# Group norm by tile, its first weight slab split in the last chunk, and low halves of the normed outputs on GpSimd

## The chip, the cores and the metric

The kernel runs on one core of a Trainium2 chip. The metric is the device time of one execution in microseconds. Before the change three runs gave 1732.81, 1736.08 and 1736.42 us, a median of 1736.08 us.

## The reference, cut to what matters

A two-layer decoder trunk over 272 tokens (16 learned meta tokens and 256 of text) of 1024 features: sliding-window attention and a dense SwiGLU, then RWKV-7 time mixing and a top-2-of-8 mixture of experts; a layer norm follows each of the four. The change concerns the end of the RWKV-7 mixer:

```
y = wkv7_scan(r, decay, k, v, -kk, kk * a)          # 16 heads of 64
mu_y  = mean(y, -1); var_y = mean((y - mu_y)^2, -1) # per head and token
y = ((y - mu_y) * rsqrt(var_y + GN_EPS)).reshape(B, L, D)
y = y * lnx_g + lnx_b
bonus = sum(r * k * r_k, -1) * v
return ((y + bonus) * g) @ w_o
```

Only the 256 text tokens are needed from here on. All values are float32, and the output is held to float32 accuracy.

## The kernel before, in words

**Layout.** Features lie on the 128 partitions in 8 tiles (`KC`); a tile of the text tokens is 128 x 256. One tile holds two heads. Weights come in slabs of 128 x 2048 (1 MB, 16 tiles of 128 x 128) through a ring of 7 slots in SBUF, which SyncE's queue fills in order (L413); slot n % 7 is loaded again once `slab_taken` says that slab n was split.

**Products in three parts.** A weight slab and the activations are each split in a rounded high half (`_hi`, type float32r) and a low half (`_lo`, the value less its high half). For each slab ScalarE makes `w_hi` by a copy (`round_slab`), VectorE makes `w_lo` by a subtraction (`split_slab`), both in two buffers (n % 2), and TensorE (`products`) runs for each of the 16 tiles w_hi with x_hi and w_hi with x_lo, then waits for `w_lo` and runs w_lo with x_hi for the 16 tiles. That is 48 matmuls of a slab. `linear` walks over the slabs of a square 1024 x 1024 product: 4 slabs, each with two output tiles m and the 8 input tiles k of each, in the order m, then k. For m = 0 it waits for the low half of input tile k before it is used. The same `linear` serves the attention's output projection.

**The recurrence.** RWKV-7 runs over 5 chunks (16 tokens, then four times 64). `recurrence_order()` writes out by hand, once for all engines, the order of the products (TensorE, counted by `c_pe`), of the steps on VectorE (`c_dve`), the copies out of PSUM on ScalarE (`c_act`) and the masks on GpSimd (`c_pool`); the arrays PT, DV, AV and PV give each step's count. The parts of a chunk are "first", five "level" (the doubling of a triangular inverse), "x", "sa", "y" and "s"; the last chunk has "bonus0" and "bonus1" between "x", "sa" and "y" and no "s". The parts of one chunk's end and of the next one's start alternate. Each part works in halves of four tiles (g = 0, 1). The output y is written over the tensor `r_`, the bonus times v into `z`, and the gate g lies in `g_`. `w_hi` and `w_lo` lie over buffers of the recurrence, so a slab can be rounded only once the chunks are done with these.

**Group norm and output projection, before.** After the last copy of y, in this order:
1. ScalarE rounds slab `SL_O2`, VectorE splits it; meanwhile TensorE makes the per-head means of all 8 tiles (`head_sums`, L795, 8 matmuls, one increment).
2. VectorE subtracts the means from all of y in one instruction of 128 x 2048; ScalarE squares all of it in one (L1297); TensorE sums the squares of each head in 8 matmuls with 16 output rows (`head_rows`, L802).
3. VectorE adds epsilon on 16 x 256 (L1713), ScalarE takes the root (L1299), VectorE the reciprocal (L1715); TensorE spreads the 16 rows to all features in 8 matmuls that read 16 rows (`rows_to_features`, L808, one increment at the end).
4. For each tile k, VectorE multiplies by the weight and the spread root (L1721), adds the bias and the bonus (L1723), multiplies by the gate, and makes the low half of tile k - 1; ScalarE makes the high halves (L1303). TensorE starts `linear` on `SL_O2` as tiles come.
5. The residual, the layer norm, the router and the experts follow, all behind this product.

In the profile TensorE matmul instructions of float32 operands have two records each; those of float32r have one.

Of the kernel before, what the change touches and what calls it, by code (L numbers as in the profile page):

```python
# [149 lines left out]
GN_OUT = 3  # L150
# [9 lines left out]
def build(nc, A, OUT):  # L160
    ctx = ExitStack()
    with ctx:
# [124 lines left out]
        b_ra, k_ra, bk_nat = pair[0:2], pair[2:4], pair[4:6]  # L287
        mrb, ltm = [x[:, 0] for x in b_ra], [x[:, 1] for x in b_ra]
# [99 lines left out]
        gn_dve, gn_act, gn_pe = sem("gn_vector_steps"), sem("gn_scalar_steps"), sem("gn_sums")  # L388
        rt_pe, rt_dve, rt_act = sem("router_products"), sem("router_vector_steps"), sem("router_scalar_steps")
# [45 lines left out]
        def _(pool):  # L435
# [50 lines left out]
            for part, c, *level in order:  # L486
# [38 lines left out]
        def _(pe):  # L525
# [20 lines left out]
            def linear(base, outs, chunks, x_hi, x_lo, ready, kept=None, before_out=0, cols=slice(0, T)):  # L546


                for n in range(base, base + outs * chunks // TILES):
                    tiles = [divmod((n - base) * TILES + t, chunks) for t in range(TILES)]  # L550

                    def before(t):
                        m, k = tiles[t]
                        if k == 0 and kept is not None and m + before_out >= 8:
                            pe.wait_ge(kept, m + before_out - 7)
                        if m == 0:
# [3 lines left out]
                                           for t, (m, k) in enumerate(tiles)], before=before)  # L560
# [230 lines left out]
            def head_sums(square, x, wait, value, done):  # L791

                pe.wait_ge(wait, value)
                for m in range(KC):
                    mm = pe.matmul(PS[:, m, TEXT], square, x(m), start=True, stop=True)  # L795
                mm.then_inc(done, 1)

            def head_rows(wait, value, done):

                pe.wait_ge(wait, value)  # L800
                for m in range(KC):
                    mm = pe.matmul(PS[0:HEADS, 0, TEXT], to_head[:, m, :], sq[:, m, TEXT], start=m == 0, stop=m == KC - 1)  # L802
                mm.then_inc(done, 1)

            def rows_to_features(wait, value, done):
                pe.wait_ge(wait, value)
                for m in range(KC):
                    mm = pe.matmul(PS[:, m, TEXT], from_head[:, m, :], rstd[0:HEADS, TEXT], start=True, stop=True)  # L808
                mm.then_inc(done, 1)
# [131 lines left out]

            pe.wait_ge(c_dve, len(DV))
            head_sums(mean_head[:, :], lambda m: r_[:, m, TEXT], c_act, len(AV), gn_pe)
            head_rows(gn_act, 1, gn_pe)
            rows_to_features(gn_dve, 3, gn_pe)
# [144 lines left out]
        def _(act):  # L1090
# [177 lines left out]
            for part, c, *level in order:  # L1268
# [9 lines left out]
                for g in range(2):  # L1278
# [12 lines left out]
                    kept = kept + 1  # L1291
            assert kept == len(AV)
            act.wait_ge(c_dve, len(DV))
            act.wait_ge(c_pe, len(PT))
# [3 lines left out]
            act.wait_ge(gn_dve, 2)  # L1298
            act.activation(rstd[0:HEADS, TEXT], rstd[0:HEADS, TEXT], ACT.Sqrt).then_inc(gn_act, 1)  # L1299
            round_slab(SL_O2 + 1)  # L1300
            for k in range(KC):
                act.wait_ge(gn_dve, GN_OUT + 3 * (k + 1))
# [78 lines left out]
        def _(dve):  # L1381
# [254 lines left out]
            steps = []  # L1636

# [13 lines left out]
            for part, c, *level in order:  # L1651
# [35 lines left out]
                elif part == "level":  # L1687
                    kinds = slice(0, 2) if i < len(levels_of(c)) - 1 else slice(1, 2)
                    for g in range(2):
# [4 lines left out]
                                ALU.add))  # L1694
                elif part[:-1] == "bonus":
# [3 lines left out]
                    step(tt(z[:, 4 * i:4 * i + 4, TEXT], PS[:, 0:4, TEXT], v_[:, 4 * i:4 * i + 4, TEXT]))  # L1699
                elif part == "s":  # L1700
# [3 lines left out]
            dve.wait_ge(c_dve, len(DV))  # L1704

            s = Steps(gn_dve)
            y = r_[:, :, TEXT]
            dve.wait_ge(c_pe, len(PT))
# [284 lines left out]
```

## Time and profile before

| | |
|---|---|
| median of three runs | 1736.08 us (1732.81 to 1736.42) |
| the profiled execution | 1734.36 us, with a span of 1732.6 us |
| TensorE matmul, busy | 1634.2 us (94%), 12050 records |
| VectorE busy | 1289.9 us (74%) |
| ScalarE busy | 999.6 us (58%) |
| GpSimd busy | 92.8 us (5%) |
| granted TensorE clock, mean | 0.962 |
| from the last y product to the layer norm behind the output projection | 628.3 to 690.2 us in the span |
| the experts | from about 734 us to the end |

The share of busy time is a mean over very different stages. The stage that the change touches takes some 62 us of the span; it has to be read by itself, in the table of stretches and in the chain of waits.

### The profile page before, as it was taken

To read this page: it belongs to the slowest core of one execution; us is meant where nothing else is said; L and a number is where in the kernel's file an instruction comes from. 1 tells how busy PE (TensorE), PEld (TensorE's weight loads), DVE (VectorE), ACT (ScalarE), POOL (GpSimd) and SP (SyncE) were. 2 spreads that over 40 slices of the span, in tenths; PEclk is the share of its full clock that TensorE was granted. 3 is DMA by queue.
4 is the path that set the end of the run, shared out by engine and by line. 5 is a ranking of instruction groups with operands and counts; after the bars stand their busy time and mean duration, and the time that the engine had idled before them with its cause. 6 is when DMAs were issued, how large, how long until landed. Compare 5 with 4: busy or idle time off the path is not lost.

```text
span 1732.6 us, 29765 instructions
## 1 busy us (share of the span) xinstructions
PE 1634.2 (94%) x12050; PEld 1288.7 (74%) x12050; DVE 1289.9 (74%) x1260; ACT 999.6 (58%) x1037; POOL 92.8 (5%) x125
## 2 busy tenths in 40 slices
PE   7998999979999977799999999999999999999995
PEld 5787999949889967677777777776777777777774
DVE  3755554466744444789899898998998998998984
ACT  3645443336512221577777777777777777777773
POOL 3310000000023400000000000000000000000000
PEclk9988999989899987799999999999999999999997
DMA  9432454513300002179999999999999999999980
GB/s 260 179 122 99 175 182 185 200 49 119 126 3 4 4 26 76 55 298 369 371 359 366 371 360 371 361 367 369 359 371 373 354 369 369 361 370 360 370 315 26
DMA packets 60291, 425.40 MB, mean 246 GB/s; under 512 B 6887, under 2 KB 8023, under 8 KB 9224
## 3 DMA queue, kind: packets, MB, share of 16 engines
q1 hardware_dynamic: 58152, 416.52, 63.3%
q0 software_dynamic: 2016, 7.13, 1.6%
q8 instruction: 90, 1.47, 0.3%
q14 instruction: 33, 0.27, 0.0%
HBM read 422.28 MB, written 1.12 MB: 244 GB/s over the span
## 4 chain that ended last, share of the span: by engine, by line
PE 71%; DVE 3%; ACT 2%; issue 1%; ACTq 0%; DVEq 0%
PE PS L530 54%; PE PS L817 5%; PE PS L531 4%; PE PS L1035 1%; PE PS L836 1%; PE PS L991 1%; PE PS L845 1%; DVE arena L1396 1%; PE PS L570 1%; PE PS L1021 0%; PE PS L1022 0%; PE PS L576 0%; PE PS L808 0%; PE PS L959 0%; PE PS L802 0%
## 5 line engine op out<-in xcount | busy, mean ns | idle before, releaser
L1396 DVE TENSOR_TENSOR w_lo<-ring,w_hi 128x2048 fp32r<-128x2048 f32 x391 | 894.2, 2288 | 200.3 <-ACT w_hi L1325 88.1
L1325 ACT ACTIVATE w_hi<-ring 128x2048 fp32r<-128x2048 f32 x336 | 644.6, 1919 | 264.3 <-PE PS L530 241.7
L530 PE MATMUL PS<-w_hi,x_hi 128*96 128x512 f32 x896 | 353.9, 395 | 0.7 <-ACT x_hi L1317 0.7
L530 PE MATMUL PS<-w_hi,x_lo 128*96 128x512 f32 x896 | 352.5, 393 | 0.0
L530 PE MATMUL PS<-w_lo,x_hi 128*96 128x512 f32 x896 | 243.0, 392 | 0.0
L1096 ACT ACTIVATE w_hi<-ring 128x2048 fp32r<-128x2048 f32 x55 | 105.3, 1914 | 168.2 <-issue 89.9
L530 PEld LDWEIGHTS PS<-w_lo,x_hi 128*96 128x96 f32 x896 | 144.6, 161 | 62.1
L530 PEld LDWEIGHTS PS<-w_hi,x_lo 128*96 128x96 f32 x896 | 144.8, 162 | 58.5
L530 PEld LDWEIGHTS PS<-w_hi,x_hi 128*96 128x96 f32 x896 | 144.6, 161 | 57.9 <-ACT x_hi L1317 1.0
L530 PE MATMUL PS<-w_hi,hid_hi 128*96 128x512 f32 x448 | 176.7, 394 | 0.0
L530 PE MATMUL PS<-w_hi,hid_lo 128*96 128x512 f32 x448 | 176.0, 393 | 0.0
L530 PE MATMUL PS<-w_lo,hid_hi 128*96 128x512 f32 x448 | 121.9, 394 | 0.0
L817 PE MATMUL PS<-arena 64*64 64x64 f32 (+4 forms) x3296 | 104.1, 216 | 6.2 <-DVE arena L1396 2.3
L1290 ACT ACTIVATE arena<-PS 128x256 f32<-128x256 f32 (+2 forms) x82 | 31.8, 393 | 135.4 <-PE PS L817 83.5
L817 PEld LDWEIGHTS PS<-arena 64*64 64x64 f32 (+2 forms) x3296 | 98.2, 131 | 11.4 <-issue 6.3
L531 PE MATMUL PS<-h_hi,w_hi 128*128 128x272 f32 x352 | 91.9, 295 | 6.8 <-DVE h_lo L1396 6.8
L1396 DVE TENSOR_TENSOR arena<-arena,PS 128x272 f32<-128x272 f32 (+6 forms) x102 | 54.3, 534 | 56.2 <-PE PS L817 53.9
L530 PEld LDWEIGHTS PS<-w_lo,hid_hi 128*96 128x96 f32 x448 | 72.2, 161 | 31.7
L530 PEld LDWEIGHTS PS<-w_hi,hid_hi 128*96 128x96 f32 x448 | 72.2, 161 | 30.8
L530 PEld LDWEIGHTS PS<-w_hi,hid_lo 128*96 128x96 f32 x448 | 72.3, 161 | 30.7
L531 PE MATMUL PS<-h_lo,w_hi 128*128 128x272 f32 x352 | 91.3, 292 | 0.0
L1396 DVE TENSOR_TENSOR experts<-experts,PS 96x512 f32<-96x512 f32 (+1 forms) x113 | 76.0, 673 | 0.0
(261 smaller groups left out, 2051.8 us busy)
## 6 DMA issues: line engine op xcount, KB each, us to landing
ring<-in_slabs SPq DMA_DIRECT2D x395, 1024.0 KB, 4.9
arena<-in_lora POOLq DMA_DIRECT2D x1, 1152.0 KB, 5.4
h<-in_h SPq DMA_DIRECT2D x1, 1088.0 KB, 5.2
arena<-bias_lines POOLq DMA_DIRECT2D x1, 1056.0 KB, 19.6
arena<-bias_lines POOLq DMA_DIRECT2D x1, 1040.0 KB, 24.1
arena<-in_lora POOLq DMA_DIRECT2D x1, 1024.0 KB, 11.9
out<-h SPq DMA_DIRECT2D x1, 1024.0 KB, 4.7
arena<-in_lora POOLq DMA_DIRECT2D x1, 512.0 KB, 6.5
```

Of the source, the lines that this page charges most:

```text
L530: return pe.matmul(out, x, w, start=start, stop=stop) if tokens_stay else \
L531: pe.matmul(out, w, x, start=start, stop=stop)
L570: mm = pe.matmul(PS[:, 0, cols], ones_d[:, :], z[:, k, cols], start=k == 0, stop=k == KC - 1)
L817: mm = pe.matmul(PS[64 * p:64 * p + n_out, b + g, at:at + width], lhsT(m, p), rhs(m, p), start=i == 0, stop=i == len(pairs) - 1)
L836: mm = pe.matmul(out[64 * p:64 * p + CH, :, 0:n], rows_of(x, c)(m, p), r_kk[64 * p:64 * p + 64, :, T * m + START[c]:T * m + START[c] + n], ...
L845: mm = pe.matmul(PS[64 * p:64 * p + CH, b + g, col + CH * (m % 4):col + CH * (m % 4 + 1)], x(m, p), masks[64 * p:64 * p + 64, MASKS.index( ...
L991: mm = pe.matmul(PS[:, 2 * (j % 4) + i, 0:HALF], rows[:, t, P * k:P * k + P], pick[:, t, 4 * half:4 * half + 4, :].rearrange("p e c -> p ( ...
L1035: mm = pe.transpose(PS[:, 4 + g % 2, CAP * j:CAP * (j + 1)], hid_rows[0:CAP, g % 2, P * j:P * (j + 1)], eye[0:CAP, 0:CAP])
L1096: act.activation(w_hi[:, n % 2, :], ring[:, n % SLOTS, :], ACT.Copy).then_inc(hi_set, 1)
L1290: act.activation(out, rows, ACT.Copy).then_inc(c_act, 1)
L1325: act.activation(w_hi[:, n % 2, :], ring[:, n % SLOTS, :], ACT.Copy).then_inc(hi_set, 1)
L1396: tt = lambda o, a, b, op=ALU.mult: dve.tensor_tensor(out=o, in0=a, in1=b, op=op)
```

## The change

On **TensorE**, `head_sums`, `head_rows` and `rows_to_features` become one function `group_norm`: the mean of tile m waits only for its half of y and signals by itself; the sum of squares takes each tile as it is squared; the spreading signals tile by tile. `linear` takes the tiles of a product's first slab in the order k, then m, where the product has fewer than 16 input tiles (this holds for the attention's output projection too). On **ScalarE**, slab `SL_O2` is rounded in quarters after the copies of the last three levels of the last chunk; the squares are taken tile by tile. On **VectorE**, `SL_O2` is split after the last level of the last chunk; (bonus + lnx_b) * g is made in place in `z` right behind each bonus step; the means are subtracted tile by tile; for each tile there are two instructions in place of four: gated y times weight times root, and the sum with `z`. The split of `SL_O2 + 1` moves behind the last of them. On **GpSimd** there are 8 products y * g (into `gated_y`, over the space of `kk`) and 8 subtractions for the low halves `out_lo`.

```diff
@@ pool, behind the recurrence @@
+            for m in range(KC):
+                pool.wait_ge(gn_dve, GN_NORMED + m)
+                pool.tensor_tensor(out=gated_y[:, m, TEXT], in0=r_[:, m, TEXT], in1=g_[:, m, TEXT], op=ALU.mult)\
+                    .then_inc(gn_pool, 1)
+            for k in range(KC):
+                pool.wait_ge(gn_dve, gn_out(k))
+                pool.wait_ge(out_hi_set, k + 1)
+                pool.tensor_tensor(out=out_lo[:, k, TEXT], in0=r_[:, k, TEXT], in1=out_hi[:, k, TEXT].bitcast(F32),
+                                   op=ALU.subtract).then_inc(out_split, 1)
             pool.wait_ge(slab_used, SL_MOE)
@@ tensor, linear @@
-                    tiles = [divmod((n - base) * TILES + t, chunks) for t in range(TILES)]
+                    tiles = [(t, *divmod((n - base) * TILES + t, chunks)) for t in range(TILES)]
+                    if n == base and chunks < TILES:
+                        tiles.sort(key=lambda x: (x[2], x[1]))
@@ tensor, in place of head_sums, head_rows, rows_to_features @@
+            def group_norm():
+                pe.wait_ge(c_dve, len(DV))
                 for m in range(KC):
+                    pe.wait_ge(c_act, AV["y", N_CH - 1, 0, m // 4])
+                    pe.matmul(PS[:, m, TEXT], mean_head[:, :], r_[:, m, TEXT], start=True, stop=True).then_inc(gn_pe, 1)
                 for m in range(KC):
+                    pe.wait_ge(gn_act, m + 1)
                     mm = pe.matmul(PS[0:HEADS, 0, TEXT], to_head[:, m, :], sq[:, m, TEXT], start=m == 0, stop=m == KC - 1)
+                mm.then_inc(gn_pe, 1)
+                pe.wait_ge(gn_dve, GN_ROOT)
                 for m in range(KC):
+                    pe.matmul(PS[:, m, TEXT], from_head[:, m, :], rstd[0:HEADS, TEXT], start=True, stop=True)\
+                        .then_inc(gn_pe, 1)
...
+            group_norm()
+            pe.wait_ge(gn_dve, gn_scaled(1))
             linear(SL_O2, 8, KC, lambda k: out_hi[:, k, TEXT], lambda k: out_lo[:, k, TEXT], (out_split, lambda k: k + 1),
@@ scalar @@
+                if part == "level" and c == N_CH - 1 and i >= 2:
+                    act.wait_ge(c_pe, PT["s", N_CH - 2, 0, 1])
+                    for j in ((), (), (0, 1), (2,), (3,))[i]:
+                        round_quarter(SL_O2, j)
...
-            round_slab(SL_O2)
-            act.wait_ge(gn_dve, 1)
-            act.activation(sq[:, :, TEXT], r_[:, :, TEXT], ACT.Square).then_inc(gn_act, 1)
+            for m in range(KC):
+                act.wait_ge(gn_dve, GN_NORMED + m)
+                act.activation(sq[:, m, TEXT], r_[:, m, TEXT], ACT.Square).then_inc(gn_act, 1)
@@ vector @@
+            def gated_bonus(i):
+                dve.wait_ge(c_dve, DV["bonus", N_CH - 1, i, 0])
+                for m in range(4 * i, 4 * i + 4):
+                    gn.mark(dve.scalar_tensor_tensor(out=z[:, m, TEXT], in0=z[:, m, TEXT], scalar=v_of("lnx_b", m),
+                                                     in1=g_[:, m, TEXT], op0=ALU.add, op1=ALU.mult))
...
+                    if c == N_CH - 1 and i == len(levels_of(c)) - 1:
+                        dve.wait_ge(c_pe, PT["u", c, i, 1])
+                        split_slab(SL_O2)
...
+                    gated_bonus(i)
...
-            split_slab(SL_O2)
-            dve.wait_ge(gn_pe, 1)
-            s.step(tt(y, y, PS[:, :, TEXT], ALU.subtract))
+            for m in range(KC):
+                dve.wait_ge(gn_pe, m + 1)
+                gn.mark(tt(r_[:, m, TEXT], r_[:, m, TEXT], PS[:, m, TEXT], ALU.subtract))
...
+            def scale(k):
+                dve.wait_ge(gn_pool, k + 1)
+                dve.wait_ge(gn_pe, KC + 2 + k)
+                gn.mark(dve.scalar_tensor_tensor(out=r_[:, k, TEXT], in0=gated_y[:, k, TEXT], scalar=v_of("lnx_g", k),
+                                                 in1=PS[:, k, TEXT], op0=ALU.mult, op1=ALU.mult))
+            scale(0)
+            for k in range(KC):
+                if k + 1 < KC:
+                    scale(k + 1)
+                dve.wait_ge(gn_dve, gn_scaled(k))
+                gn.mark(tt(r_[:, k, TEXT], r_[:, k, TEXT], z[:, k, TEXT], ALU.add))
             split_slab(SL_O2 + 1)
-            for k in range(KC):
-                yk = r_[:, k, TEXT]
-                s.step(dve.scalar_tensor_tensor(out=yk, in0=yk, scalar=v_of("lnx_g", k), in1=PS[:, k, TEXT],
-                                                op0=ALU.mult, op1=ALU.mult))
-                s.step(dve.scalar_tensor_tensor(out=yk, in0=yk, scalar=v_of("lnx_b", k), in1=z[:, k, TEXT],
-                                                op0=ALU.add, op1=ALU.add))
-                s.mark(tt(yk, yk, g_[:, k, TEXT]))
-                if k:
-                    dve.wait_ge(gn_dve, s.n - 3)
-                    left(out_lo[:, k - 1, TEXT], r_[:, k - 1, TEXT], out_hi[:, k - 1, TEXT], out_hi_set, k, out_split)
```

## Rows read from the trace of the kernel before

**Rows 1.** Stretches: length; busy PE, PEld, DVE, ACT, POOL; granted clock; DMA share; GB/s.
```profile
628.00:633.00 5.00, 3.96 (x26) 3.08 (x22) 2.30 (x2) 2.18 (x2) 0.00 (x0) 1.00 0.00 0
633.00:637.00 4.00, 0.00 (x0) 0.00 (x0) 2.18 (x1) 1.78 (x1) 0.00 (x0) 0.89 0.67 236
...
646.40:653.60 7.20, 7.16 (x16) 5.14 (x16) 2.29 (x1) 0.01 (x1) 0.00 (x0) 0.50 0.42 146
653.60:667.10 13.50, 4.78 (x13) 3.01 (x12) 12.85 (x31) 3.24 (x8) 0.00 (x0) 0.50 0.00 0
667.10:671.10 4.00, 3.96 (x20) 3.82 (x21) 0.43 (x1) 0.10 (x1) 0.00 (x0) 0.60 0.00 0
671.10:690.20 19.10, 19.10 (x163) 19.10 (x162) 6.66 (x8) 3.83 (x2) 0.00 (x0) 1.00 0.31 111
900.00:1700.00 800.00, 800.00 (x3630) 566.06 (x3628) 727.66 (x454) 577.97 (x381) 0.00 (x0) 1.00 0.94 358
```

**Rows 2.** Chain of waits in order of time: start us, us, what.
```profile
632.99 2.21 DVE arena L1396
...
635.22 1.92 ACT sq L1297
...
637.18 6.47 PE PS L802 x16
...
644.64 1.75 DVE rstd L1715
...
646.44 7.21 PE PS L808 x16
...
653.67 0.49 DVE arena L1721
...
667.13 23.07 PE PS L531 x180
```

**Rows 3.** Timeline of the last chunk: start us, us, engine, line, what.
```profile
609.41 0.85 ACT L1290 ACTIVATE arena<-PS 128x256 f32<-128x256 f32 x2 [4.05 <-PE PS L817]
...
618.20 0.42 DVE L1396 TENSOR_TENSOR arena<-arena,PS 128x256 f32<-128x256 f32 x1 [0.28 <-PE PS L817]
...
621.98 1.23 DVE L1396 TENSOR_TENSOR z<-PS,arena 128x1024 f32<-128x1024 f32 x1 [3.36 <-PE PS L934]
...
625.36 1.22 DVE L1396 TENSOR_TENSOR z<-PS,arena 128x1024 f32<-128x1024 f32 x1 [2.15 <-PE PS L934]
...
628.31 0.38 ACT L1290 ACTIVATE arena<-PS 128x256 f32<-128x256 f32 x1 [0.96 <-PE PS L817]
...
628.84 3.69 PE L795 MATMUL PS<-arena,mean_head 128*128 128x256 f32 x16 [0.57 <-ACT arena L1290]
```

**Rows 4.** Timeline of the later layer norm, eight tiles in a row.
```profile
693.70 2.73 DVE L1428 TENSOR_TENSOR z<-z,PS 128x256 f32<-128x256 f32 x8 [2.70 <-PE PS L570]
...
701.07 3.25 DVE L1434 SCALAR_TENSOR_TENSOR z<-z,vec,rstd 128x256 f32<-128x256 f32 x8
```

**Rows 5.** Timeline: the same kind of sums over heads, earlier.
```profile
450.50 3.84 PE L746 MATMUL PS<-z,spare 128*16 128x272 f32 x16
```

**Rows 6.** Timeline: VectorE and GpSimd at the same time.
```profile
609.29 0.42 DVE L1396 TENSOR_TENSOR arena<-arena,wc 128x256 f32<-128x256 f32 x1
...
609.46 0.83 POOL L509 TENSOR_TENSOR arena<-arena,spare 128x256 f32<-128x256 f32 x1 [3.49 <-PE PS L817]
609.62 0.95 DVE L1396 TENSOR_TENSOR arena<-arena,wc 128x256 f32<-128x256 f32 x1
```

**Rows 7.** Groups of instructions: busy us, mean ns; idle before.
```profile
L1303 ACT ACTIVATE out_hi<-arena 128x256 fp32r<-128x256 f32 x8 | 3.3, 417 | 17.5 <-DVE arena L1396 17.5
```

**Rows 8.** Groups on GpSimd, whole span.
```profile
L509 POOL TENSOR_TENSOR arena<-arena,spare 128x256 f32<-128x256 f32 x40 | 30.7, 792 | 33.4 <-PE PS L817 33.4
L475 POOL TENSOR_TENSOR w_lo<-ring,w_hi 128x512 fp32r<-128x512 f32 x16 | 20.4, 1275 | 37.8 <-ACT w_hi L1103 34.0 <-issue 3.8
```

**Rows 9.** Table of stretches: the attention's output projection, first slab.
```profile
101.60:106.40 4.80, 4.80 (x33) 4.80 (x32) 0.32 (x1) 0.30 (x1) 0.00 (x0) 0.79 0.07 26
```

More of the change, by code:

```diff
@@ L149, with gn_scaled, gn_out @@
 RT_SEL, RT_EXP, RT_POS, RT_FLAG, RT_GATES = 7, 9, 10, 12, 18
-GN_OUT = 3
+GN_NORMED, GN_SUM, GN_ROOT = 9, 17, 18
+def gn_scaled(k):
+    return GN_ROOT + (1 if k == 0 else 2 * k)
+def gn_out(k):
+    return GN_ROOT + (2 * k + 3 if k < KC - 1 else 2 * KC)
 LN_READY = 10
@@ L549, in linear, with before @@
                 for n in range(base, base + outs * chunks // TILES):
-                    tiles = [divmod((n - base) * TILES + t, chunks) for t in range(TILES)]
-                    def before(t):
-                        m, k = tiles[t]
+                    tiles = [(t, *divmod((n - base) * TILES + t, chunks)) for t in range(TILES)]
+                    if n == base and chunks < TILES:
+                        tiles.sort(key=lambda x: (x[2], x[1]))
+                    def before(i):
+                        _, m, k = tiles[i]
                         if k == 0 and kept is not None and m + before_out >= 8:
@@ L559, in linear @@
                     products(n, n % 2, P, [(t, x_hi(k), x_lo(k), PS[:, m, cols], k == 0, k == chunks - 1)
-                                           for t, (m, k) in enumerate(tiles)], before=before)
+                                           for t, m, k in tiles], before=before)
             def layer_norm(l):
@@ L1715, in _ @@
-            s.step(dve.reciprocal(rstd[0:HEADS, TEXT], rstd[0:HEADS, TEXT]))
-            split_slab(SL_O2 + 1)
-            dve.wait_ge(gn_pe, 3)
-            assert s.n == GN_OUT
-            for k in range(KC):
-                yk = r_[:, k, TEXT]
-                s.step(dve.scalar_tensor_tensor(out=yk, in0=yk, scalar=v_of("lnx_g", k), in1=PS[:, k, TEXT],
-                                                op0=ALU.mult, op1=ALU.mult))
-                s.step(dve.scalar_tensor_tensor(out=yk, in0=yk, scalar=v_of("lnx_b", k), in1=z[:, k, TEXT],
-                                                op0=ALU.add, op1=ALU.add))
-                s.mark(tt(yk, yk, g_[:, k, TEXT]))
-                if k:
-                    dve.wait_ge(gn_dve, s.n - 3)
-                    left(out_lo[:, k - 1, TEXT], r_[:, k - 1, TEXT], out_hi[:, k - 1, TEXT], out_hi_set, k, out_split)
@@ L1729, in _ @@
-            dve.wait_ge(gn_dve, s.n)
-            left(out_lo[:, KC - 1, TEXT], r_[:, KC - 1, TEXT], out_hi[:, KC - 1, TEXT], out_hi_set, KC, out_split)
+            for m in range(KC):
+                dve.wait_ge(gn_pe, m + 1)
+                gn.mark(tt(r_[:, m, TEXT], r_[:, m, TEXT], PS[:, m, TEXT], ALU.subtract))
+            dve.wait_ge(gn_pe, KC + 1)
+            gn.mark(dve.tensor_scalar(rstd[0:HEADS, TEXT], PS[0:HEADS, 0, TEXT], 1.0 / HD, GN_EPS, ALU.mult, ALU.add))
+            assert gn.n == GN_SUM
@@ new lines, in _ @@
+            dve.wait_ge(gn_act, KC + 1)
+            gn.mark(dve.reciprocal(rstd[0:HEADS, TEXT], rstd[0:HEADS, TEXT]))
+            def scale(k):
[3 more added lines that the diff above has]
+                                                 in1=PS[:, k, TEXT], op0=ALU.mult, op1=ALU.mult))
+                assert gn.n == gn_scaled(k)
```

32 lines of the change are left out of this document (6 added, 26 removed).

## The prediction, written before the result was known

> **What bounds the kernel now.** I read the table of stretches first, because the page's means mix stages. In the experts TensorE is busy 800.00 of 800 us at full clock [rows 1]: whatever the group norm ends earlier, all that follows starts and ends earlier by as much. Nothing but TensorE's own order sets the end there, so only the 62 us from the last y product to the layer norm matter. There TensorE is idle from 632.5 to 637 (0.00 busy of 4.00), works at a granted clock of 0.50 (the 1.2 GHz level) from 646.4 to 667.1, and from 653.6 is busy only 4.78 of 13.50 us, while VectorE has 12.85 [rows 1]. The chain of waits says in which order: one wide subtraction (2.21), one wide square (1.92), sums of squares over heads (6.47), reciprocal (1.75), spreading (7.21), then VectorE's loop over tiles from 653.67 until TensorE can run on at 667.13 [rows 2]. That loop advances (667.13 - 653.67) / 8 = 1.68 us a tile: three instructions in a chain and the low half of the tile before.
>
> **The sum, part by part.** Times are of the profiled execution (1734.36 us, span 1732.6).
>
> 1. *The slab's rounding and split in the last chunk: hidden.* ScalarE has copies at 609.41 and then free time; four quarters are together about one rounding (the 2.18 us of ScalarE between 628 and 633 hold it) and fall into gaps of at least 1 us behind three levels [rows 1, 3]. VectorE's last level step starts at 618.20 and ends at 618.62, its next step at 621.98 waits for TensorE: a split of 2.29 us ends at 620.95, 1.0 us before [rows 3]. If that cover were gone, the chain would be late by what the split runs over, at most 2.3 us. The ring slot is freed some 12 us earlier; the queue's DMA share is 0.00 between 628 and 633, and the new transfer meets nothing [rows 1].
>
> 2. *The bonus part: hidden.* Eight instructions of two SBUF operands at 0.40 us each (3.25 / 8, [rows 4]) stand in two fours behind the bonus steps. The first four run from 623.2 to 624.9, before the second bonus step can start at 625.4; the second four from 626.6 to 628.3, when TensorE still works on y [rows 3]. Cost between 0 and 0.5 us, taken as 0.
>
> 3. *Means.* Tiles 0 to 3 wait only for the half of y copied earlier, so the 8 matmuls start at 628.3, not 628.84, and take 3.69 us [rows 3]: they end at 632.0. VectorE's subtractions of a tile take 0.34 (2.73 / 8, [rows 4]), less than the 0.46 of a mean, so the last ends at 632.5 and its square at 633.0.
>
> 4. *Sums of squares.* TensorE goes straight on at 632.0 and needs the last square only at 635.2. The same kind of sums, busy without a pause at full clock, took 3.84 us for 272 columns [rows 5], so 3.6 for 256, against 6.47 now [rows 2]. They end at 635.6, against 643.65: 8.0 us saved so far, 5.2 by the order and 2.9 by the clock.
>
> 5. *Root and reciprocal* are unchanged: 646.44 - 643.65 = 2.8 us [rows 2]. Spreading starts at 638.4. Here TensorE is idle, and the trace shows the clock still full through the first 3 us of an idle stretch and at 0.50 after it (0.89 in the mean of 633 to 637) [rows 1]. During spreading it stayed at 0.50 although the engine was busy 7.16 of 7.20 us [rows 1]. So the clock will fall while spreading runs, not at its start. The ends are 3.7 us (as long as the means at full clock) and 7.21; the middle, 5.4, puts its end at 643.8. It signals tile by tile, so VectorE can begin at 639.1.
>
> 6. *Products with the gate on GpSimd: hidden.* 8 of 0.79 us [rows 8], one after the other from 629.4, end by 635.8; the first is needed at 639.1. The subtractions read PSUM and one SBUF tensor.
>
> 7. *The loop.* VectorE has 0.40 + 0.34 = 0.74 us a tile [rows 4], ScalarE one copy of 0.42 [rows 7], GpSimd a subtraction of 0.79 (0.72 by half of the 1.275 for 512 columns plus a fixed part) [rows 8]. GpSimd and VectorE are not independent: beside a GpSimd instruction VectorE's took 0.95 instead of 0.42 us and ended 0.28 behind it [rows 6]. VectorE's sum of two SBUF tensors and GpSimd's subtraction therefore take turns: 0.72 + 0.27 = 1.0 us a tile. The bounds are 0.74 (no hindrance) and 1.78 (0.83 and 0.95 one behind the other); I take 1.0, as the two rows overlap. The first sum starts at 639.9 and the last at about 646.5 (the first tiles are unhindered, the later ones 1.0 apart); with the copy and the subtraction the last low half would be there 1.7 later, at 648.2.
>
> The split of the next slab (2.29 us, two SBUF operands) now stands right behind the last sum. GpSimd's last subtraction can't start until ScalarE's copy is there, 0.9 us later, and by then VectorE has begun the split: the last low half comes at 650.4. By the Trainium skill, SBUF — State Buffer, section "SBUF: two separate sides", the port pair that VectorE and GpSimd share is held for a whole instruction and the other is blocked fully; the trace agrees (0.95 for 0.42), and without the rule the price of the split would be 0 instead of 2.2 us.
>
> 8. *TensorE's first slab.* With both output tiles of each k taken together, 4 matmuls follow each tile. At 20 matmuls in 3.96 us at a clock of 0.60 [rows 1], four take 0.85 at 0.50. From 643.8 tiles 0 to 6 take until 649.8, the last waits for 650.4 and ends at 651.0 (between full and half clock). Most of GpSimd's delay is thus hidden by TensorE's half clock. Today this pass ends at 671.1: **20.1 us saved**. Before the change 16 of its matmuls came only behind the last tile; they now stand in the loop's gaps.
>
> 9. *The rest of the projection*, 160 matmuls, took 19.10 us at full clock [rows 1]. The clock came back about 3 us after the work became dense (667.13; a mean of 0.60 up to 671.1) [rows 1, 2]. If it is late, the pass with w_lo costs 16 x 0.1 = 1.6 more; I take 0.5. The split of the second slab, done by about 649.5 to 652, is needed behind its 32 first matmuls, at 656: hidden.
>
> 10. *The attention's projection* also gets the new order. TensorE was busy 4.80 of 4.80 us in its first slab [rows 9]: no wait to fill, 0.
>
> Sum: -20.1 + 0.5 = -19.6 us, 1734.36 - 19.6 = 1714.8 for an execution like the profiled one. The median shown is 1.7 above it, which would give 1716.5. I take the middle of the four readings, 1735.2: **1715.6 us**.
>
> **Rivals.**
> - *Half clock for long (20%).* The clock falls as spreading begins (7.2 us, to 645.6), all of the first pass runs at half (6.8, to 652.4), and w_lo's too (+1.6): 17.1 saved, 1718.1. For it: 0.50 from 646.4 to 667 in spite of partly busy stretches [rows 1]. Against: TensorE now idles only 2.8 us. By the Trainium skill, TensorE: Matmul & The Clock Gate, section "HAM oscillation — how this bites in real kernels", gaps in TensorE's work lower the clock and the work after them starts cold; the trace shows it in this stage.
> - *GpSimd in VectorE's way at every tile (8%).* At 1.78 us a tile the last low half is at 639.85 + 1.5 + 7 x 1.78 = 653.8, the pass ends at 654.7, the clock is late: 1.6 more. 14.8 saved, 1720.4. The Trainium skill, GPSIMD Engine Reference, section "Engine selection", advises against GpSimd for elementwise work of two inputs, at about twice VectorE's time; the row (0.79 against 0.42) agrees, and it is the reason why the pace could be GpSimd's.
> - *No hindrance (15%).* Loop at 0.74, full clock: the last low half is at 639.85 + 7 x 0.74 + 1.5 = 646.5, the pass ends at 647.0, 24.1 saved: 1711.1.
> - *The clock does not come back (2%), slower.* Each us of TensorE's work at 0.50 costs half a us; the 19.6 saved are used up after 39 us at the low level, more than the whole projection. With 50 us it would be 1740.6. Against: in this stage dense work brought 1.00 at 671 [rows 1].
> - *The change doesn't free the chain (5%).* If the quarters, the split or the bonus instructions disturb the last chunk, its chain is late by a few us; for no change it would have to be 16 us or more, out of all gaps in [rows 3]. Part of it (2 to 5 us) gives 1718 to 1721; whole, 1735.
>
> **How the numbers follow.** The forecast has the other 50%, with its own range from 1713 to 1718.5 (spreading 3.7 to 7.2, the pass's end 650 to 652.5, 1 us between runs). Two in ten left out, the range is 1711 to 1720.5. A measurement tells 0.2%, 3.5 us, from nothing. Faster takes all cases but the clock that stays low and most of the last one: 0.95; same 0.03; slower 0.02.
>
> **What would show it.** In the trace after: a split of 2.29 us at 618.7 and the bonus step still at 622.0 (step 1); TensorE without a pause from the means through the sums of squares, these in 3.6 us (3, 4); 2.8 us to the spreading, which changes its matmul time midway (5); low halves 1.0 us apart, the last 3 us behind the one before (7); all tiles of the first pass done at 651 (8). Wrong would be: the last low half before 649 with the split beside it, low halves over 1.3 us apart, or a stretch of the projection at 0.50 longer than 5 us.

## The result and the profile after

| | before | changed |
|---|---|---|
| median, first measurement | 1736.25 us (1732.81 to 1738.40, 4 runs) | 1712.75 us (1710.11 to 1720.65, 4 runs) |
| ratio, first measurement | | 0.9874, 95% interval 0.9838 to 0.9910 |
| median, second measurement | 1733.12 us (11 runs) | 1717.24 us (6 runs) |
| ratio, second measurement | | 0.9907, interval 0.9890 to 0.9923 |
| profiled execution, span | 1734.36 us, 1732.6 us | 1712.69 us, 1710.9 us |
| from the first mean to the layer norm's sums | 61.20 us | 40.96 us |

The kernel is faster by 23.5 us in one measurement and by 15.9 in the other, 19.7 in the mean; 19.6 was predicted. The two measurements lie 7.6 us apart, so it is partly luck that their mean falls on the prediction. The last line of the table is steadier than the whole time: the second profiled execution of the changed kernel has 40.95 us there, though its span is 5.0 us longer. I use this stretch as the measure of all experiments. It isn't free of chance either: in both these executions TensorE's clock fell 2.7 us into the spreading, and in other runs it fell elsewhere (below). The stretch is counted from the start of the first mean matmul to the start of the first matmul of the layer norm's sums.

The table of stretches of the changed kernel, with the columns of [rows 1]:

```profile
628.00:633.00 5.00, 5.00 (x42) 3.86 (x39) 4.04 (x10) 3.52 (x9) 3.19 (x5) 1.00 0.01 3
632.20:635.90 3.70, 3.65 (x17) 1.47 (x16) 0.56 (x3) 0.97 (x3) 3.13 (x5) 1.00 0.02 4
636.00:638.50 2.50, 0.00 (x0) 0.00 (x0) 2.02 (x2) 2.17 (x2) 0.00 (x0) 1.00 0.00 0
638.50:643.10 4.60, 4.53 (x17) 3.32 (x17) 3.74 (x11) 1.30 (x4) 1.88 (x3) 0.80 0.00 0
643.10:650.40 7.30, 6.22 (x32) 6.02 (x32) 6.24 (x8) 2.08 (x5) 6.82 (x6) 0.66 0.00 0
650.55:669.60 19.05, 19.05 (x163) 19.05 (x162) 6.66 (x8) 3.83 (x2) 0.00 (x0) 1.00 0.44 163
900.00:1680.00 780.00, 779.10 (x3533) 551.11 (x3531) 708.05 (x441) 563.12 (x373) 0.00 (x0) 1.00 0.93 358
```

Where TensorE was idle for 4 us between means and sums [rows 1], it is now busy 5.00 of 5.00 and then 3.65 of 3.70 us. Its long pause is the root and reciprocal (636 to 638.5). One more stands in the view of waits of this kernel (who waited for whom, us in total, times, longest), ahead of the last tile:

```profile
PE PS L550 <- POOL out_lo L534: 1.1, 1, 1.1
```

The clock is at 0.50 for part of the spreading and of the first pass (means of 0.80 and 0.66), instead of for over 20 us. From 650.55 on it is the same work as before, 160 matmuls in 19.1 us at 1.00, and the experts are still TensorE's (779.10 of 780).

The chain of waits, against [rows 2]:

```profile
628.64 3.65 PE PS L817 x16
632.29 3.57 PE PS L820 x16
...
636.78 1.75 DVE rstd L1739
...
638.57 0.71 PE PS L824 x2
...
640.20 0.43 DVE arena L1412
...
646.32 0.78 POOL out_lo L534
...
647.19 2.74 POOL out_lo L534
...
649.97 19.72 PE PS L550 x164
669.69 3.47 PE PS L591 x16
```

The wide subtraction and the wide square are gone from it; the sums take 3.57 instead of 6.47 us. The loop appears as GpSimd's eight subtractions (two of them shown), with the first beginning at 641.2 and the last alone lasting 2.74 us. Behind that 164 matmuls stand, where there were 180 in [rows 2].

The timeline of the last chunk, against [rows 3]:

```profile
618.58 0.42 DVE L1412 TENSOR_TENSOR arena<-arena,PS 128x256 f32<-128x256 f32 x1 [0.28 <-PE PS L833]
618.91 2.28 DVE L1412 TENSOR_TENSOR w_lo<-ring,w_hi 128x2048 fp32r<-128x2048 f32 x1
...
622.36 1.23 DVE L1412 TENSOR_TENSOR z<-PS,arena 128x1024 f32<-128x1024 f32 x1 [1.16 <-PE PS L950]
...
623.62 1.67 DVE L1659 SCALAR_TENSOR_TENSOR z<-z,vec,arena 128x256 f32<-128x256 f32 x4
...
625.73 1.23 DVE L1412 TENSOR_TENSOR z<-PS,arena 128x1024 f32<-128x1024 f32 x1 [0.44 <-PE PS L950]
626.99 1.67 DVE L1659 SCALAR_TENSOR_TENSOR z<-z,vec,arena 128x256 f32<-128x256 f32 x4
...
628.57 3.72 PE L817 MATMUL PS<-arena,mean_head 128*128 128x256 f32 x16
...
629.31 3.44 DVE L1412 TENSOR_TENSOR arena<-arena,PS 128x256 f32<-128x256 f32 x8 [0.64 <-PE PS L817]
...
629.80 5.53 POOL L529 TENSOR_TENSOR arena<-arena 128x256 f32<-128x256 f32 x8 [16.01 <-DVE arena L1412]
```

The split (618.91, 2.28 us) lies in VectorE's gap, and the bonus step at 622.36 still starts when TensorE lets it. The two fours of gated bonus are 1.67 us each. GpSimd's eight products with the gate take 5.53 us beside means and sums.

### The profile page after: what moved, and what is told of

Read it like the earlier page. It is cut to its first block, busy times and chain, and to the rows that moved or that the text cites. A ratio compares the mean times of both kernels' runs of the same rounds, so it can differ in the third digit from the quotient of the medians.

```text
span 1710.9 us, 29796 instructions
## 1 busy us (share of the span) xinstructions
PE 1625.2 (95%) x12050; PEld 1285.2 (75%) x12050; DVE 1288.7 (75%) x1259; ACT 1001.3 (59%) x1047; POOL 106.7 (6%) x141
## 4 chain that ended last, share of the span: by engine, by line
PE 72%; DVE 2%; ACT 1%; issue 1%; POOL 0%; ACTq 0%; DVEq 0%; POOLq 0%
PE PS L549 54%; PE PS L833 5%; PE PS L550 4%; PE PS L852 1%; PE PS L1049 1%; PE PS L1005 1%; PE PS L861 1%; DVE arena L1412 1%; PE PS L591 1%; PE PS L1035 1%; POOL out_lo L534 0%; PE PS L1036 0%; PE PS L597 0%; PE PS L973 0%; ACT h L1129 0%
## 6 DMA issues: line engine op xcount, KB each, us to landing
arena<-bias_lines POOLq DMA_DIRECT2D x1, 1056.0 KB, 19.6
```

## The experiments

Each one is the changed kernel with one edit (more where it is said), and was profiled once. The stretch from the first mean to the layer norm's sums is the measure; in brackets stands the ratio of the whole time to the kernel before, which ran beside it. The last four ran on another chip than the eight before them.

One thing has to be known for all of them. The clock fell to 0.50 at different places: 1.1 to 3.3 us into the spreading in nine of the thirteen executions of the changed kernel and its variants, but 0.3 to 0.7 us before the first matmul of the spreading in the other four, while TensorE was idle. These four are, in this order, the low halves on VectorE, the old order, the last low half on VectorE, and the products with the gate in the loop (columns of [rows 1]):

```profile
640.58:640.94 0.36, 0.00 (x0) 0.00 (x0) 0.32 (x1) 0.34 (x1) 0.00 (x0) 0.50 0.00 0
641.94:642.42 0.48, 0.00 (x0) 0.00 (x0) 0.43 (x1) 0.46 (x1) 0.00 (x0) 0.50 0.00 0
642.40:643.05 0.65, 0.00 (x0) 0.00 (x0) 0.63 (x1) 0.65 (x1) 0.00 (x0) 0.50 0.00 0
640.08:640.38 0.30, 0.00 (x0) 0.00 (x0) 0.30 (x2) 0.28 (x1) 0.00 (x0) 0.50 0.00 0
```

None of their edits touches what TensorE does between the last chunk and that place. In these four the spreading took 7.19 us, and where GpSimd makes the low halves, the first began 3.6 us after the spreading's start instead of 2.6. So by my estimate about 1 us of such a run's stretch comes from where the clock fell and not from its edit, and more where the clock also came back later.

**The changed kernel again**, the second measurement above.

> The changed kernel once more, beside the kernel before on the same chip, as the measure for the experiments run with it. Both theories: ratio to the kernel before 0.986 to 0.990; the stretch from the first mean to the layer norm's sums 41.0 us, give or take 1.5 us for where in the spreading the clock falls and when it returns.

40.95 us, against 40.96 in the first profile; 1717.24 us (0.9907, 0.9890 to 0.9923). Its span is 5.0 us longer because the first mean starts at 633.57 instead of 628.57. Of that, 2.6 us are there when the attention's projection starts (102.4 and 99.8), ahead of everything that the change touches, and 3.6 us at the first layer norm (its sums start at 128.51 and 124.88). So whole times of the same kernel differ by some 4 us between measurements, and tenths of a per cent can't be read from them.

**Split of the second slab behind the last low half.**

```diff
+            dve.wait_ge(out_split, KC)
             split_slab(SL_O2 + 1)
```

> The split of the projection's second slab waits for the eighth low half, all else as in the changed kernel. Theory (VectorE's instruction of two SBUF tensors and GpSimd's exclude each other): GpSimd's last subtraction, 2.74 us in the changed kernel, falls to 0.6 to 0.8 us and ends at about 647.9 instead of 649.93; TensorE's wait of 1.08 us before the last tile goes, because its first pass is then bound by its own half clock (tile 6 ended at 648.9); the split ends at about 650.3 and is not waited for. The stretch from the last y product to the layer norm's sums (41.0 us) shrinks by 0.9 to 1.2 us. Rival (the last subtraction was long for a reason of its own, as the wait for ScalarE's copy): it stays near 2.7 us and the stretch at 41.0.

39.63 us, 1.33 less; 1715.37 us (0.9892, 0.9875 to 0.9908). The two instructions that met in the changed kernel, VectorE's split and GpSimd's last subtraction, in its timeline:

```profile
646.52 2.82 DVE L1412 TENSOR_TENSOR w_lo<-ring,w_hi 128x2048 fp32r<-128x2048 f32 x1
...
647.19 2.73 POOL L534 TENSOR_TENSOR out_lo<-arena,out_hi 128x256 fp32r<-128x256 f32 x1
```

In this kernel the split starts later (timeline), and none of GpSimd's eight subtractions (the view of the tile `out_lo`: shortest, median and longest in ns) lasts over 0.87 us:

```profile
650.42 2.29 DVE L1412 TENSOR_TENSOR w_lo<-ring,w_hi 128x2048 fp32r<-128x2048 f32 x1 [1.35 <-POOL out_lo L534]
```

```profile
L534 POOL TENSOR_TENSOR out_lo<-arena,out_hi x8: 727/868/873, 643.7 to 649.7; 128x256 fp32r<-128x256 f32 x8
```

The split is back at 2.29 us from 2.82, the last subtraction at 0.87 from 2.73. The theory of mutual exclusion holds, the rival falls. The last low half is there 9.3 us after the spreading's start, not 11.4. TensorE's wait before the last tile is gone; of the 2.0 us, 0.7 are lost again behind the last low half, since TensorE, at 0.50 up to 650.2, hasn't caught up with the tiles by then.

**Low halves back on VectorE.**

```diff
+                if k:
+                    dve.wait_ge(gn_dve, gn_out(k - 1))
+                    left(out_lo[:, k - 1, TEXT], r_[:, k - 1, TEXT], out_hi[:, k - 1, TEXT], out_hi_set, k, out_split)
...
-                pool.tensor_tensor(out=out_lo[:, k, TEXT], in0=r_[:, k, TEXT], in1=out_hi[:, k, TEXT].bitcast(F32),
-                                   op=ALU.subtract).then_inc(out_split, 1)
```

> The eight low halves go back to VectorE, each behind the next tile's sum; the products y * g stay on GpSimd. Theory (TensorE at half clock, 0.85 us a tile, covers most of what the loop costs): VectorE's loop is 0.40 + 0.34 + 0.34 = 1.1 to 1.2 us a tile, last low half at 649.5 to 650, close to the 649.93 of the changed kernel, in which the split holds it up; the stretch of 41.0 us changes by less than 0.7 us. Rival (the move to GpSimd is what brought the gain): the loop is back at 1.5 us or more a tile and the stretch is 3 to 5 us longer.

41.20 us, 0.24 more; 1715.42 us (0.9890, 0.9873 to 0.9906). The loop runs at 1.06 us a tile. As far as this run shows, the last part of the title, the low halves on GpSimd, is worth nothing measurable. The pace of 0.87 instead of 1.06 us gives seven times 0.19, which is 1.3 us, and the last subtraction, held up by the split, takes 1.9 us more. But like isn't compared with like. This is one of the four runs with the early fall of the clock: from the spreading's end TensorE ran 192 matmuls without a pause in 24.17 us, so the loop wasn't its limit. The last low half came 10.8 us after the spreading's start, sooner than in the changed kernel (11.4), and sooner still against the run with the old order, whose clock fell as early (12.4). So the low halves on GpSimd may have cost something as the change stands, by up to 1.6 us in the loop; what the stretch would be with the later fall was not measured.

**The slab late, as in the kernel before.**

```diff
+            act.wait_ge(c_dve, len(DV))
+            act.wait_ge(c_pe, len(PT))
+            round_slab(SL_O2)
...
+            dve.wait_ge(c_pe, len(PT))
+            split_slab(SL_O2)
             for m in range(KC):
                 dve.wait_ge(gn_pe, m + 1)
```

> Slab SL_O2 is rounded and split behind the last copy of y again, all else as in the changed kernel. Theory (the split stands ahead of the subtractions on VectorE, so it is on the path): rounding 628.7 to 630.6, split to 632.9, subtractions by 0.34 us to 635.6, squares to 636.1; TensorE, done with the means at 632.3, waits for the first square until about 633.8 and ends the sums at about 637.3 instead of 635.9; the stretch grows by 1.3 to 2.5 us. Rival (hidden, since the means cover it): no change, below 0.5 us.

43.15 us, 2.2 more; 1717.94 us (0.9904, 0.9888 to 0.9921). The chain of this kernel (first mean at 632.52):

```profile
634.91 2.29 DVE w_lo L1411
637.20 0.34 DVE arena L1411
...
637.56 0.43 ACT sq L1312
...
638.03 3.64 PE PS L820 x16
```

The split is in it, with the first subtraction and square behind it. TensorE's sums start 1.9 us later behind the start of the means than in the changed kernel (5.51, not 3.65): the theory, not the rival. The other 0.3 us lie behind the last low half, where the clock comes back late.

**Old order of the first slab's tiles.**

```diff
-                    if n == base and chunks < TILES:
-                        tiles.sort(key=lambda x: (x[2], x[1]))
```

> The first slab's tiles are taken in the old order again (both projections). Theory: 16 matmuls instead of 2 pairs stand behind the last tile; the seven tiles before take only half of TensorE's time, which idles in the loop; 14 matmuls more behind 649.97 cost 14 x 0.12 = 1.7 us at full clock and up to 3 us if the clock is still at its half level, which is likelier with the idle time. The attention's projection starts as before within 0.1 us. Rival (nothing, since the loop and not TensorE is the bound): below 0.5 us.

45.46 us, 4.5 more; 1719.28 us (0.9914, 0.9897 to 0.9930). The sign is the theory's, the size is above its bound of 3 us. But 1.0 us isn't the order's. Behind the last tile it has 178 matmuls in 23.17 us, the changed kernel 164 in 19.72. The clock is 0.50 from 0.5 us before the spreading up to 658 and 0.75 in the mean of 658 to 660, 4 us after the last low half; in the changed kernel it is back before the last tile. 14 matmuls at 0.12 us are 1.7 of the 4.5; 1.0 lies ahead of the last low half (12.4 us after the spreading's start, not 11.4) and is that of the early fall; the rest, 1.8, is the late clock. That TensorE's waits in the loop delay the clock is the likely reason and was not tried by itself. The early fall alone doesn't explain it: in the two runs that have it with the new order and without the gate's products in the loop, the clock was back 10.2 and 13.7 us after it fell, here 17.1. In the attention's projection it does nothing: from its start to the layer norm's sums this kernel takes 26.1 us, as the changed one in its second profile; 25.1 in the first, like the kernel before.

**Each step of the norm waits for the whole of the one before.**

```diff
+            dve.wait_ge(gn_pe, KC)
             for m in range(KC):
-                dve.wait_ge(gn_pe, m + 1)
...
+                pe.wait_ge(gn_act, KC)
```

> The same instructions by tile, but each step waits for the whole of the step before: the first subtraction for all means, the first square for all subtractions, the first sum for all squares. Theory (the order by tile saves twice: the pauses, and the full clock for the sums): TensorE idles 632.3 to about 638.8 on the changed kernel's times, 6.3 us for subtractions (2.8) and squares (2.8) and their starts; the clock falls in it, and the sums take 6.4 instead of 3.6 us: the stretch grows by 7.5 to 9.5 us (41 to 49 or 50). Rival (the clock stays up, only the pauses count): sums in 3.6 us and 6.3 to 6.6 us more. Second rival (hidden by the rest): below 2 us.

48.05 us, 7.1 more; 1721.74 us (0.9929, 0.9910 to 0.9948). This lies between the theory's 7.5 to 9.5 and the first rival's 6.3 to 6.6, so the stretches have to decide. Here are the idle time and the sums (columns of [rows 1]).

```profile
635.40:640.80 5.40, 0.04 (x1) 0.00 (x0) 2.74 (x8) 2.55 (x8) 4.82 (x8) 0.99 0.00 0
640.80:646.10 5.30, 5.22 (x16) 1.83 (x16) 0.00 (x0) 0.01 (x1) 0.69 (x2) 0.69 0.01 3
```

The idle time is 5.4 us, since subtractions and squares need 2.75 and 2.57, and the sums take 5.22 instead of 3.63: the clock comes back in their midst (0.69). So the pauses make 5.4 and the clock 1.6: the theory, with pauses shorter than it had.

**Unused matmuls before the spreading.**

```diff
+                for m in range(6):
+                    pe.matmul(PS[:, 7, T:T + 240], mean_head[:, :], r_[:, m, N_META:256], start=True, stop=True)
                 pe.wait_ge(gn_dve, GN_ROOT)
```

> Six matmuls of 240 columns whose output is not used stand in TensorE's idle time between the sums of squares and the spreading (2.7 us); the output of the kernel is the same. Theory (what the clock costs here is mostly hidden by VectorE's and GpSimd's loop, only what TensorE does behind the loop counts): the clock falls later or not at all, spreading and first pass go quicker, but the last low half stays near 649.9, so the stretch of 41.0 us changes by less than 1 us. Rival 1 (the idle time is what costs): clock 1.00 up to the projection's end, the stretch 2 us or more shorter. Rival 2 (the spreading itself, which reads 16 rows, lets the clock fall): the clock still falls during or after the spreading.

40.97 us, no change; 1714.77 us (0.9886, 0.9867 to 0.9905). The clock falls as in the run of the changed kernel beside it, to means of 0.55 and 0.56 between 646 and 648: the first rival, that the clock stays up once the idle time is filled, is out. The theory, that the clock is covered by the loop, is not tested, since the clock did not change; the second rival is what happened. Whether the filled idle time keeps off the early fall isn't settled: the three runs that fill it don't have one, but neither do six of the ten that leave it idle.

**The same and one unused matmul behind each of seven spreading matmuls, split behind.**

```diff
                         .then_inc(gn_pe, 1)
+                    if m < KC - 1:
+                        pe.matmul(PS[:, 7, T:T + 240], mean_head[:, :], sq[:, m, N_META:256], start=True, stop=True)
```

> The split of the second slab behind the last low half, the six unused matmuls before the spreading, and one more behind each of the first seven spreading matmuls. Theory: clock 1.00 from the means to the projection's end; low halves 0.87 us apart, the last about 9.4 us after the spreading's start; TensorE then has only the last tile and the w_lo pass, so the stretch from the first mean to the layer norm is 38.6 to 39.4 us: 1.6 to 2.4 less than the changed kernel and 0.3 to 1.1 less than with the split moved alone (39.7). In the whole time this is 0.1%, at the edge of what is measured. Rival (the added matmuls delay the spreading's signals and with them the loop): the loop paced at 0.93 us and more, the stretch 40 us or more.

48.22 us, 7.3 more; 1723.02 us (0.9941, 0.9921 to 0.9961): a miss. Its stretches up to the first pass:

```profile
630.30:640.20 9.90, 9.88 (x46) 6.60 (x44) 5.57 (x11) 5.88 (x11) 5.53 (x8) 1.00 0.01 2
640.20:654.40 14.20, 14.12 (x31) 6.29 (x31) 5.77 (x14) 2.55 (x7) 4.31 (x6) 0.62 0.00 0
```

TensorE is busy 9.88 of 9.90 and 14.12 of 14.20 us, and all the same the clock falls in the second stretch (0.62), 3.3 us into the spreading. There the added matmuls cost 1.1 us each, and VectorE gets a tile every 2.24 us.

**Unused matmuls of the rounded type, split behind.** There are 22 in the idle time and two behind each of the first seven spreading matmuls.

```diff
+                pe.wait_ge(hi_set, SL_O2 + 1)
+                for m in range(22):
+                    pe.matmul(PS[:, 7, T:T + 240], w_hi[:, SL_O2 % 2, 0:P], w_hi[:, SL_O2 % 2, P:P + 240], start=True, stop=True)
                 pe.wait_ge(gn_dve, GN_ROOT)
...
+                    for i in range(2 if m < KC - 1 else 0):
+                        pe.matmul(PS[:, 7, T:T + 240], w_hi[:, SL_O2 % 2, 0:P], w_hi[:, SL_O2 % 2, P:P + 240], start=True, stop=True)
```

> The split behind the last low half, and unused matmuls of the rounded type (240 columns of the slab's high half, full clock 0.12 us each): 22 in the idle time before the spreading, 2 behind each of its first seven. With unused float32 matmuls in the same places the clock fell although TensorE had no pause, and each tile of the spreading took 2.24 us. Theory A (it is the kind of matmul that lets the clock fall): now it stays at 1.00; spreading paced at 0.70 us a tile, low halves 0.87 apart, the stretch 38.6 to 39.4 us. Theory B (the spreading of 16 rows pulls the clock down whatever stands between): it falls to 0.50 in the spreading, which then takes about 1.3 us a tile, and the stretch is 41 us or more.

46.79 us, 5.8 more; 1721.69 us (0.9926, 0.9913 to 0.9940). Stretches as above:

```profile
631.40:641.30 9.90, 9.90 (x56) 6.93 (x54) 5.57 (x11) 5.88 (x11) 5.53 (x8) 1.00 0.01 2
641.30:653.30 12.00, 11.92 (x31) 6.40 (x30) 6.41 (x14) 2.56 (x7) 3.89 (x6) 0.62 0.00 0
```

Again no pause, and again a fall (at 644.2, 2.8 us into the spreading): of the two theories B. The tiles come 1.86 us apart at the low clock, not 1.3. That it is the 16 rows, as theory B has it, isn't shown by this; it shows that neither a pause nor the kind of the added matmuls is needed for the fall.

**Last low half on VectorE.**

```diff
-            for k in range(KC):
+            for k in range(KC - 1):
                 pool.wait_ge(gn_dve, gn_out(k))
...
+            dve.wait_ge(out_split, KC - 1)
+            left(out_lo[:, KC - 1, TEXT], r_[:, KC - 1, TEXT], out_hi[:, KC - 1, TEXT], out_hi_set, KC, out_split)
             split_slab(SL_O2 + 1)
```

> As the changed kernel, but VectorE makes the eighth low half itself, and only then splits the second slab; GpSimd makes the other seven. Theory (the last subtraction was only held up by the split): the eighth low half lies behind ScalarE's copy at once, 0.42 us, about 9.0 us after the spreading's start instead of 11.4; TensorE's first pass is then bound by TensorE's half clock or by this; the stretch from the first mean to the layer norm's sums is 39.3 to 40.0 us (changed kernel 41.05, split moved alone 39.7). Rival (only the wait of GpSimd mattered and VectorE gets no better): 40.5 or more.

42.59 us, 1.6 more; 1715.69 us (0.9889, 0.9874 to 0.9904). By its number the rival; but the stretch doesn't decide. The last low half took 0.43 us on VectorE and was there 10.2 us after the spreading's start, 1.2 earlier than in the changed kernel (11.4) and 2.2 earlier than in the run with the old order (12.4), whose clock fell as early: so far the theory. In this execution the clock fell 0.7 us before the spreading, which took 7.19 instead of 4.6 us, and came back 13 us after its start; TensorE ran from the spreading's end without a pause and needed 25.56 us for 192 matmuls. What is gained on VectorE is hidden by TensorE at 1.2 GHz then. The run with the split behind the last low half met the milder case (4.92 us), so its 1.33 us hold for that case.

**The products with the gate in VectorE's loop.**

```diff
+                tt(gated_y[:, k, TEXT], r_[:, k, TEXT], g_[:, k, TEXT]).then_inc(gn_pool, 1)
                 dve.wait_ge(gn_pool, k + 1)
```

> The eight products y * g go from GpSimd, where they lay beside the means, into VectorE's loop, as one more instruction of two SBUF tensors for each tile. Theory (taking turns with GpSimd's subtraction sets the pace): 0.72 + 2 x 0.27 = 1.26 us and with the wait for the product 1.3 to 1.4 us a tile instead of 0.87; the last low half 3.0 to 3.7 us later; the stretch of 41.05 us becomes 43.5 to 45. Rival (TensorE's half clock hides it): less than 1 us more.

47.51 us, 6.5 more; 1722.73 us (0.9933, 0.9917 to 0.9949), well above the 2.5 to 4 expected. The last low half came 5.0 us later than in the changed kernel, where 3.0 to 3.7 were expected; some 1.0 of it is that of the clock's early fall. One tile of its loop in the timeline:

```profile
646.49 0.41 DVE L1408 TENSOR_TENSOR arena<-arena 128x256 f32<-128x256 f32 x1
...
646.94 0.48 DVE L1741 SCALAR_TENSOR_TENSOR arena<-arena,vec,PS 128x256 f32<-128x256 f32 x1
647.16 0.73 POOL L530 TENSOR_TENSOR out_lo<-arena,out_hi 128x256 fp32r<-128x256 f32 x1 [0.87 <-ACT out_hi L1315]
647.34 0.83 DVE L1408 TENSOR_TENSOR arena<-arena,z 128x256 f32<-128x256 f32 x1
```

A tile takes 1.60 us: product (646.49), scaling (646.94) and sum (647.34), the sum 0.83 instead of 0.42 us as it stands against GpSimd (647.16). The low half and the next product wait in turn. The seventh subtraction is held up by the split (2.52 us), and the clock, back at 650.3, was at 0.50 once more from 657.2 to 660.6, after TensorE had waited three times for tiles (3.8 us in all). That lies behind the last low half, where this run needs 1.5 us more than the changed kernel.

**The old loop.**

```diff
-            for m in range(KC):
-                pool.wait_ge(gn_dve, GN_NORMED + m)
...
+            dve.wait_ge(gn_pe, 2 * KC + 1)
+            for k in range(KC):
+                yk = r_[:, k, TEXT]
+                gn.step(dve.scalar_tensor_tensor(out=yk, in0=yk, scalar=v_of("lnx_g", k), in1=PS[:, k, TEXT],
+                                                 op0=ALU.mult, op1=ALU.mult))
...
```

> The norm by tile and the early slab stay, but the loop is the old one: spreading waited for as a whole, four instructions a tile on VectorE with the low half among them, no gated bonus ahead, nothing on GpSimd. Theory (the loop is about half of the gain): spreading's start as now, 9.9 us after the first mean; spreading 4.6 to 7.2 us, then 14.1 us as in the kernel before to the last low half, at 29 to 31 us instead of 21.3; behind it 19.7 us and 1 to 2 us of half clock: the stretch is 50 to 53 us. Rival (most of the gain is in the norm by tile and the early slab, the loop is hidden by TensorE): 45 us or less.

50.37 us, 9.4 more; 1726.42 us (0.9956, 0.9940 to 0.9971). This undoes several things at once: four instructions a tile on VectorE, no gated bonus ahead, nothing on GpSimd, the spreading awaited as a whole, and the second slab's split ahead of the loop as in the kernel before. The loop's stretch:

```profile
646.30:659.70 13.40, 7.31 (x24) 5.58 (x24) 12.80 (x31) 3.25 (x8) 0.00 (x0) 0.50 0.13 54
```

VectorE is busy 12.80 of 13.40 us, TensorE 7.31, at 0.50. The loop with the gated bonus ahead is about half of the gain (9.4 of 20.2 us), as the theory said.

## Why the prediction was right

- Steps 1 and 2 (hidden): as said, to within the 0.4 us by which the last chunk's steps come later (618.58 for 618.20, 622.36 for 621.98). Undone, the early slab costs 2.2 us.
- Steps 3 and 4: sums from 632.2 to 635.9 at full clock; predicted 632.0 to 635.6. With the steps whole it costs 7.1 us; the sum had 8.0.
- Step 5: 2.7 us to the spreading, which took 4.59, with the clock falling in its midst; I took 5.4 as the middle. The place of the fall was the uncertain thing, and the runs have 4.4 to 7.2. That the clock falls only while the spreading runs is no rule, as I made it from one idle stretch: in four runs it had fallen before, after 2.0 to 2.4 us of idle time. This is the condition of the rival "half clock for long", to which I gave 20%. That both profiles of the changed kernel have the milder case is partly luck. The rival put 2.5 us on it; the run with the last low half on VectorE has 42.59 us, against 39.63 with the split behind, which keeps the last low half from waiting too but had the later fall: 3.0 us.
- Step 6: 5.53 us, not 6.3. It ends at 635.3 and is hidden. What it adds is nothing, as the sum had it; what it takes from the loop stands in step 7. If it is put into the loop the stretch is 6.5 us longer, of which some 1.0 is that of the clock's early fall.
- Step 7: 0.87 us a tile, not 1.0; the last low half at 649.93, not 650.4. The split held up GpSimd as foreseen, and moved away it gives back 1.33 us. The chance of 15% for no hindrance was too large: from the third tile on VectorE's sums take 0.56 for 0.42 us.
- Step 8: the first pass ends at 650.55, predicted 651.0. TensorE was at half clock through it, as expected, but got it back at about 648, before the last tile, so step 9's 0.5 us was not needed. Four matmuls took 0.85 us at 0.50 as said, though the row that I named for it gives 0.95 if time simply goes with the clock (3.96 x 0.60 / 20 x 4 / 0.50).
- Step 9: 19.1 us for 160 matmuls. Step 10: nothing, as predicted. The attention's projection started at 99.8 us, 1.7 us earlier than in the kernel before, but that isn't the change's: the same kernel's second profile has 102.4, and that with the old order 101.5.

From the last y product's end to the layer norm the profiles have 61.92 and 41.06 us: 20.9 saved, where the sum had 19.6. The difference of 1.3 is the first pass, which ended 0.5 us sooner than predicted, the 0.5 us of step 9, and the last y product, which ended 0.3 us later than before. The rest of the span's 21.7 is 1.2 us behind this stretch, less 0.3 ahead of it.

The parts undone one at a time give 2.2 (slab), 7.1 (steps), 9.4 (loop) and 4.5 (order): 23.2 together, for 20.2. 1.0 of the 4.5 is that of the clock's early fall. The rest of the excess I put down to an overlap in TensorE's clock, which was not tested: each part that makes TensorE wait also puts more of its work at 0.50.

Not settled: a version better than the changed one. The split behind the last low half is ahead by 1.33 us in the stretch of one profile, but its 1715.37 us (0.9892) lie between the two values of the changed kernel. Nor is it settled whether GpSimd or VectorE should make the low halves, since the run that compares them had the early fall.

## What to carry to other kernels

When a chain passes over three engines, cut it by tile and let each tile signal; the gain is the pauses and, on TensorE, the clock that is kept. Work that doesn't depend on the late step (here the bonus times the gate, the product with the gate, the next slab's split) is worth moving out of the loop on the path: the loop as it was costs 9.4 us. A helper engine is slowed, and slows, wherever it and VectorE both read two SBUF tensors: look at what stands right behind the loop as well. And before you read a difference of 1 or 2 us from one profile, look at where the clock fell in it.

## What the runs showed of the hardware

- VectorE and GpSimd exclude each other when both read two SBUF tensors: 2.73 us for 0.87 beside a split of 2.3, and 2.82 for the split; 0.83 us for 0.42 beside a subtraction of 0.73.
- The clock fell to 0.50 about the spreading (matmuls that read 16 rows) in every run: in nine of thirteen 1.1 to 3.3 us into it, in four 0.3 to 0.7 us before it, after 2.0 to 2.4 us without work. A pause isn't needed: it also fell with the idle time filled and other matmuls put between those of the spreading, float32 ones (busy 14.12 of 14.20 us) or rounded ones (11.92 of 12.00). Whether the 16 rows are the cause was not tried by itself.
- With the steps whole it came back while the sums over heads ran, which read 128 rows and write 16 (0.69 in their mean).
- The spreading took 4.4 to 7.2 us, by where the clock fell. The whole stretch of one and the same kernel was profiled only twice, with the fall at the same place, so how much it changes the stretch of one kernel isn't measured.
